# Probabilities and values of global attention as pairs of bf16 parts, with three bf16 products in place of one float32 product

## The reference

```
def global_attention(q, k, v):
    ...
    def one_block(qi):
        logits = jnp.einsum('bqkgd,bskd->bkgqs', qi, k, preferred_element_type=jnp.float32)
        p = jax.nn.softmax(logits, axis=-1)
        return jnp.einsum('bkgqs,bskd->bqkgd', p.astype(v.dtype), v)
```

## Time and profile before

| | |
|---|---|
| median of 3 runs | 2336.33 us (2333.32 to 2338.41) |
| profiled execution, its time | 2337.93 us |
| its span, first to last instruction | 2336.1 us |
| PE busy | 2272.7 us (97%) |
| DVE busy | 1623.4 us (69%) |
| ACT busy | 1223.9 us (52%) |
| POOL busy | 1090.9 us (47%) |
| mean granted clock of TensorE | 0.992 |

### The profile page before, as it was taken

How to read it: one execution, slowest core, us unless ns; L and a number is a source line. 1 busy time by engine, 2 the same in 40 slices (tenths; PEclk the granted TensorE clock), 3 DMA queues, 4 the chain that set the end, 5 groups by cost and what they waited for, 6 DMA issues and landing times.

```text
span 2336.1 us, 55145 instructions
## 1 busy us (share of the span) xinstructions
PE 2272.7 (97%) x24026; PEld 1661.3 (71%) x24026; DVE 1623.4 (69%) x1972; ACT 1223.9 (52%) x1568; POOL 1090.9 (47%) x712
## 2 busy tenths in 40 slices
PE   8999999999999999979999999999999999999997
PEld 3554677664444458779888888888888888888874
DVE  4776666583222456867887878788878878887875
ACT  4333666583111236446566555655656656665654
POOL 0000111133332215647666677667667766766642
PEclk9999999999999999999999999999999999999998
DMA  9102201503222345568899999989999998999896
GB/s 338 38 25 73 55 2 38 181 2 91 55 54 63 100 162 157 183 251 315 307 329 341 316 338 332 323 316 340 334 318 325 344 324 314 340 332 322 321 326 251
DMA packets 252440, 524.24 MB, mean 224 GB/s; under 512 B 8412, under 2 KB 57677, under 8 KB 252077
## 3 DMA queue, kind: packets, MB, share of 16 engines
q1 hardware_dynamic: 241692, 488.51, 59.3%
q0 software_dynamic: 10512, 32.25, 4.7%
HBM read 492.42 MB, written 28.31 MB: 223 GB/s over the span
## 4 chain that ended last, share of the span: by engine, by line
PE 91%; DVE 3%; ACT 2%; issue 2%; DMA 2%; SPq 0%; POOL 0%; DVEq 0%; ACTq 0%; POOLq 0%
PE ps L1855 24%; PE ps L1857 24%; PE ps L1856 24%; PE ps L2251 4%; PE ps L2039 3%; PE ps L2051 3%; PE ps L1916 3%; PE ps L1951 1%; PE ps L2187 1%; PE ps L1892 1%; ACT arena L1087 1%; DMA arena<-w_in 1%; PE ps L1989 1%; PE ps L2216 1%; PE ps L1941 1%
## 5 line engine op out<-in xcount | busy, mean ns | idle before, releaser
L1855 PE MATMUL ps<-arena 128*128 128x160 bf16 (+4 forms) x5624 | 1388.6, 266 | 10.8 <-DVE arena L1735 7.0
L1856 PE MATMUL ps<-arena 128*128 128x160 bf16 (+4 forms) x5624 | 1389.2, 266 | 0.6 <-issue 0.6
L1857 PE MATMUL ps<-arena 128*128 128x160 bf16 (+4 forms) x5624 | 1389.3, 266 | 0.0
L1392 DVE TENSOR_TENSOR arena<-arena 128x2048 bf16<-128x2048 f32 x378 | 912.4, 2418 | 225.8 <-ACT arena L974 221.2
L974 ACT ACTIVATE arena<-arena 128x2048 bf16<-128x2048 f32 x384 | 726.6, 1904 | 218.9 <-PE ps L1857 174.6
L1855 PEld LDWEIGHTS ps<-arena 128*128 128x128 bf16 x5624 | 549.1, 98 | 162.1 <-issue 16.6
L1857 PEld LDWEIGHTS ps<-arena 128*128 128x128 bf16 x5624 | 549.1, 98 | 152.9 <-issue 0.6
L1856 PEld LDWEIGHTS ps<-arena 128*128 128x128 bf16 x5624 | 549.1, 98 | 140.7 <-issue 0.3
L868 POOL TENSOR_TENSOR arena<-arena 128x320 bf16<-128x320 f32 x128 | 262.3, 2049 | 10.0
L865 POOL TENSOR_TENSOR arena<-arena,ones 128x320 bf16<-128x320 f32 x128 | 180.9, 1413 | 143.8 <-DVE arena L1735 143.4
L1245 ACT ACTIVATE arena<-ps 128x160 f32<-128x160 f32 x256 | 77.5, 303 | 300.3 <-PE ps L1857 290.1
(11 more groups left out here) (263 smaller groups left out, 2193.2 us busy)
## 6 DMA issues: line engine op xcount, KB each, us to landing
arena<-w_e_gate SPq DMA_DIRECT2D x64, 2048.0 KB, 8.5
arena<-w_e_up SPq DMA_DIRECT2D x64, 2048.0 KB, 9.9
arena<-w_e_down SPq DMA_DIRECT2D x64, 2048.0 KB, 9.2
arena<-w_ada SPq DMA_DIRECT2D x12, 2048.0 KB, 9.2
arena<-w_in SPq DMA_DIRECT2D x30, 512.0 KB, 5.3
arena<-x_sample SPq DMA_DIRECT2D x16, 512.0 KB, 3.7
arena<-w_in SPq DMA_DIRECT2D x3, 2048.0 KB, 16.5
arena<-w_out SPq DMA_DIRECT2D x2, 2048.0 KB, 8.9
```

The source lines that it names most:

```text
L1392: ve.tensor_tensor(lo, stage_half(kind, a), hi, ALU.subtract).then_inc(lo_done, 1)
L1855: pe.matmul(out, w_hi, x_hi, start=start, stop=False)
L1856: pe.matmul(out, w_hi, x_lo, start=False, stop=False)
L1857: return pe.matmul(out, w_lo, x_hi, start=False, stop=stop)
```

## The change

V of the global branch is no longer kept as float32. ACT copies keys and V of a tile together into `raw` (256 columns in one instruction where it had two of 128), and POOL makes a high bf16 part and a low one from it, the low one being what the high one leaves. ACT waits for POOL's second instruction before it overwrites `raw` in the next tile. The turned probabilities are also kept as two bf16 parts. ACT copies all pieces of an item, rounded to bf16 (the high part), and DVE subtracts that from the same PSUM bank and writes the low part. The bank is free after the subtraction. PV of the global branch is high x high, high x low and low x high, 48 bf16 products where there were 16 float32 ones. The buffers take the same room as before. The windowed branch keeps float32 (`VB`, `PTB`).

```
--- before.py
+++ after.py
@@ -291,7 +291,7 @@
         hT = at(26112, 2, KD, P)
         qT = half_words(10240, NT, 2 * NPAIR, 2 * P)
         kT = half_words(20480, 2, 2, TOK)
-        V = at(23552, 2, NT, P)
+        VA, VB = half_words(23552, NT, 2 * P), at(24832, NT, P)
         R3, R4 = 28160, 40448
         RH = 29184
         ada_slot = {c: o for c, o in enumerate([0, 4096, 10240, 14336])}
@@ -313,7 +313,7 @@
         Pb = at(41472, 2, 2, 1024)
         PbN = at(41472, 2, 2, 256)
         PbB = at(41472, 8, 386).rearrange("p (i h) w -> p i h w", h=2)
-        PTs = [at(37376, 2, 2, 8, P), at(44560, 2, 2, 3, P)]
+        PTA, PTB = half_words(37376, 4, 8, 2 * P), at(44560, 2, 2, 3, P)
         on = [at(45568, 2, 512), at(39424, 2, 512)]
         rb = [at(23040, 512), at(40448, 512)]
         biasm = at(46592, 8, 386)
@@ -417,6 +417,7 @@
         xn_ready = sem("xn_ready")
         g_done, g_free = sem("g_done"), [sem(f"g_free{n}") for n in range(5)]
         q_in, q_sqrt, qf_ready, q_high = sem("q_in"), sem("q_sqrt"), sem("qf_ready"), sem("q_high")
+        v_in, v_high, v_split, p_high = sem("v_in"), sem("v_high"), sem("v_split"), sem("p_high")
         s_done, nm_ready, e_done = sem("s_done"), sem("nm_ready"), sem("e_done")
         b_done = sem("b_done")
         pv_done, o_norm, o_split = sem("pv_done"), sem("o_norm"), sem("o_split")
@@ -542,8 +543,7 @@
 
             return (n // 2, 4 * (n % 2)) if n_parts(items[i]) == 4 else (n, 0)
 
-        def piece_vec(i, n):
-            return len(items[i][3]) > 4 and piece(i, n)[0] == 0
+        piece_no = {x[1:]: n + 1 for n, x in enumerate(x for x in steps if x[0] == "TE" and items[x[1]][0] == 0)}
 
         def narrow(i):
             return items[i][0] == 0 and len(items[i][3]) <= 4
@@ -767,6 +767,15 @@
 
             for s in steps:
                 k = s[0]
+                if k == "G":
+
+                    t = s[1]
+                    if t == 0:
+                        gp.wait_ge(bias_out, 16)
+                    gp.wait_ge(v_in, t + 1)
+                    gp.tensor_tensor(VA[:, t, 0:P], raw[:, 640:768], ones[:], ALU.mult).then_inc(v_high, 1)
+                    gp.wait_ge(v_high, t + 1)
+                    gp.tensor_tensor(VA[:, t, P:2 * P], raw[:, 640:768], VA[:, t, 0:P], ALU.subtract).then_inc(v_split, 1)
                 if k == "RB":
                     g = s[1]
                     if g:
@@ -1023,16 +1032,17 @@
                         ac.wait_ge(g_done, 3 * t + c + 1)
                         n = 3 * t + c
                         b = ps[:, n % 5]
-                        if c:
-                            v0 = 128 if c == 1 else 384
+                        if c == 1 and t:
+                            ac.wait_ge(v_split, t)
+                        if c == 2:
                             if t == 0:
                                 ac.wait_ge(bias_out, 16)
-                            ac.activation(V[:, c - 1, t, :], b[:, v0:v0 + P], ACT.Copy)
+                            ac.activation(VB[:, t, :], b[:, 384:512], ACT.Copy)
 
                         if c == 0:
                             ins = ac.activation(raw[:, 0:512], b, ACT.Copy)
                         elif c == 1:
-                            ac.activation(raw[:, 512:640], b[:, 0:P], ACT.Copy)
+                            ac.activation(raw[:, 512:768], b[:, 0:2 * P], ACT.Copy).then_inc(v_in, 1)
                             ins = ac.activation(rawB[:, :, 0, :], b[:, 256:512].rearrange("p (j d) -> p j d", j=NPAIR),
                                                 ACT.Copy)
                         else:
@@ -1086,7 +1096,7 @@
                             p_ = src = PbB[:, i % 4, hh, slice(*window(i)[1])]
                         ac.activation(p_, src, ACT.Exp, bias=nm[:, i % 4, hh:hh + 1],
                                       accum_out=den[:, i // NPAIR % 3, 2 * j + hh:2 * j + hh + 1]).then_inc(e_done, 1)
-                if k == "TE" and not piece_vec(*s[1:]):
+                if k == "TE":
                     i, n = s[1:]
                     hh, a = piece(i, n)
                     b, free = job(("T", i, n))
@@ -1095,8 +1105,11 @@
                     if i == first_b:
                         ac.wait_ge(o_split, first_b // NPAIR)
                     z = min(4, len(items[i][3]) - a)
-                    ac.activation(PTs[items[i][0]][:, i % 2, hh, a:a + z, :], b[:, 0:z * P].rearrange("p (n q) -> p n q", n=z),
-                                  ACT.Copy).then_inc(free, 1)
+                    src = b[:, 0:z * P].rearrange("p (n q) -> p n q", n=z)
+                    if items[i][0]:
+                        ac.activation(PTB[:, i % 2, hh, a:a + z, :], src, ACT.Copy).then_inc(free, 1)
+                    else:
+                        ac.activation(PTA[:, i % 2 * 2 + hh, a:a + z, 0:P], src, ACT.Copy).then_inc(p_high, 1)
                 if k == "WS":
                     m = s[1]
                     if m == 0:
@@ -1538,15 +1551,15 @@
                         ve.tensor_tensor(p_, ps[:, 2 * (i % 2):2 * (i % 2) + 2, cols], both, ALU.add).then_inc(b_done, 1)
                         ve.wait_ge(b_done, n_add(i))
                         ve.tensor_reduce(nm[:, i % 4], p_, AX.X, ALU.max, negate=True).then_inc(nm_ready, 2)
-                if k == "TE" and piece_vec(*s[1:]):
+                if k == "TE" and items[s[1]][0] == 0:
                     i, n = s[1:]
                     hh, a = piece(i, n)
                     b, free = job(("T", i, n))
-                    if i >= 2:
-                        ve.wait_ge(pv_done, i - 1)
+                    ve.wait_ge(p_high, piece_no[(i, n)])
                     z = min(4, len(items[i][3]) - a)
-                    ve.tensor_copy(PTs[0][:, i % 2, hh, a:a + z, :], b[:, 0:z * P].rearrange("p (n q) -> p n q", n=z))\
-                        .then_inc(free, 1)
+                    p_ = PTA[:, i % 2 * 2 + hh, a:a + z]
+                    ve.tensor_tensor(p_[:, :, P:2 * P], b[:, 0:z * P].rearrange("p (n q) -> p n q", n=z), p_[:, :, 0:P],
+                                     ALU.subtract).then_inc(free, 1)
                 if k == "RB":
                     g = s[1]
                     ve.wait_ge(e_done, 2 * NPAIR * (g + 1))
@@ -2046,11 +2059,18 @@
                         pe.wait_ge(*freed[job_at[(("T", i, n), 0)]])
                     if i % NPAIR == 0 and i:
                         pe.wait_ge(o_norm, i // NPAIR)
+                    if i == 0:
+                        pe.wait_ge(v_split, NT)
                     for n, kt in enumerate(kts):
-                        for hh in range(2):
-                            ins = pe.matmul(ps[hh * 64:hh * 64 + 64, 4, j * P:(j + 1) * P],
-                                            V[:, br, kt, hh * 64:hh * 64 + 64], PTs[br][:, i % 2, hh, n, :],
-                                            start=(n == 0), stop=(n == len(kts) - 1), tile_position=(0, 64 * hh))
+                        passes = ((0, 0), (0, 1), (1, 0)) if br == 0 else ((0, 0),)
+                        for x, (u, v) in enumerate(passes):
+                            for hh in range(2):
+                                d = slice(u * P + hh * 64, u * P + hh * 64 + 64)
+                                w, m = (VA[:, kt, d], PTA[:, i % 2 * 2 + hh, n, v * P:(v + 1) * P]) if br == 0 else \
+                                    (VB[:, kt, d], PTB[:, i % 2, hh, n, :])
+                                ins = pe.matmul(ps[hh * 64:hh * 64 + 64, 4, j * P:(j + 1) * P], w, m,
+                                                start=n + x == 0, stop=n == len(kts) - 1 and x == len(passes) - 1,
+                                                tile_position=(0, 64 * hh))
                     ins.then_inc(pv_done, 1)
                 if k == "OT":
                     g = s[1]
```

1 line of the change is left out of this document (added).

## The result

| | before | after |
|---|---|---|
| median | 2336.55 us (4 runs, 2333.32 to 2338.41) | 2354.81 us (4 runs, 2353.42 to 2362.12) |
| profiled execution, its span | 2336.1 us | 2352.0 us |
| PE busy | 2272.7 us | 2261.2 us |
| DVE busy | 1623.4 us | 1665.2 us |
| ACT busy | 1223.9 us | 1254.8 us |

The changed kernel takes 1.0082 times as long, with a 95% interval of 1.0070 to 1.0094. It is slower, by 18.3 us between the medians. PE is busy 11.5 us less and the kernel is 18 us slower. The forecast was 2357 us.

The account below looks back on a forecast made before the run. PE was taken to bound the kernel (91% of the chain), its wide items only 0.19 us above a loop through other engines. Terms 23.6 - 6.4 + 2 + 1 = +20.2 us gave 2357 us, range 2346 to 2370.

Parts of the forecast that it names:

- The bound: Wide items: PE is full at 5.34 us an item, beside a loop of scores, maxima and exponentials of 5.15 us.
- PV: Probabilities times V in a wide item: 48 bf16 products take 1.64 us, where the float32 ones took 1.90.
- the rival in which the two column tiles of 64 columns queue for their loads: Wide items: weight loads share one path, the 48 products take 2.79 us, the kernel 2369 us; chance 0.17.
- Copies and subtractions: Wide items: maxima queue behind DVE's subtractions, these behind ACT's copies; ordinary items 6.02 us for 5.34, +23.6 us in all.
- AR and the small products: Wide items: PE's new free time hides most of their cost, 1.2 us left of 7.6: -6.4 us.
- the end of the stage: End of the wide items: the windowed scores wait for a DVE memset behind one more low part, +1 us (0 to 2).
- The walk: Step-by-step timing of one wide item from its maxima: next maxima at 6.02 us, 0.87 after the scores have ended.
- Narrow items: Stretch from 222 to 244 us: DVE gets 16 subtractions of 256 columns, +2 us (bounds 0 and 6.6).
- V on POOL: Projection: POOL, idle before, makes V's parts and ACT drops one copy a tile; PE covers both, 0 us.
- PE sets the pace: Wide items: DVE and ACT stay clear of PE's path, so its saving shows, -6.6 us at most, 2330 us; chance 0.06.
- No change: Whole kernel: hidden AR and saved PE time cancel a walk 0.5 us too long an item, 2337 us; chance 0.06.
- The clock: Wide items: PE's pauses lower its clock in part of the stage, 2370 us and more; chance 0.06.

Follow-up runs that it names:

- V pair: Changed kernel with V as two bf16 parts but the turned probabilities as one, two products, no subtractions, copies shared by DVE and ACT as before: 2330.20 us.
- four products: Changed kernel with the low x low product added to PV of the global branch, 64 products a wide item: 2357.09 us.
- one product: Changed kernel with PV of the global branch cut to high x high, 16 products a wide item in place of 48: 2363.06 us.
- one piece ahead: Changed kernel, same instructions, with only piece 0 turned and copied ahead of the next item's scores and maxima, piece 1 behind them: 2344.34 us.
- half the low parts: Changed kernel with low parts only for hh = 0 and high x low left out for hh = 1; ACT still makes all high parts: 2347.83 us.

## Why the prediction was right

**The bound.** Right. The loop of scores, maxima and exponentials is 5.15 us, seen bare in the V pair kernel.

**PV.** 338.79 to 340.26, 1.47 us for 48 products, 31 ns each. The term was 1.64, from 31 ns and 0.15 for a change of form, which does not appear with bf16. So the rival in which the two column tiles of 64 columns queue for their loads (2369 us) is out: it needed 2.79. The prediction took 1.64 from the loads of AR, and speaks of eight; AR has 16, of which eight fall within 0.16 us and the others, four and four, within 0.13 each. The argument held. By the Trainium skill ("TensorE: Matmul & The Clock Gate", LDWEIGHTS) 64 columns load in an estimated 53 ns; at 31 ns from product to product, the loads of the two column tiles would have to overlap. The records of these loads in the trace last 110 ns each in the median, and 48 of them lie within 1.37 us, so the records do overlap.

**Copies and subtractions.** Right, and close in size: 6.02 forecast for an ordinary item, 5.98 found from maxima to maxima (5.94 to 6.04 from scores to scores); the end of a group 7.10, found 7.06 and 7.10; a group 25.28, found 25.06, so +21.8 for eight in place of +23.6. Three experiments stand behind the reason: one piece moved in the list (-0.56 us an item), half the subtractions taken away (-0.11), and two instructions of DVE added to the kernel before (+0.5 to 1.0).

**AR and the small products.** The weakest term. Of 7.6 us I left 1.2 and added 1 for the end of the stage, 2.2; found are 203.8 - 8 x 25.06 = 3.4. The maxima, which set the pace, tell the parts: the three items with AR took 7.07, 7.08 and 7.09 us from maxima to maxima, where 5.98 is ordinary. So AR and the small products cost 3.3 us and not 1.2. The end, from the last maxima (442.71) to the windowed scores (447.86), took 5.15 us, where the forecast had 4.9. The first wide item was 0.6 us shorter than an ordinary one, which the forecast did not count, and hides a part of the error. The free time of PE was right, but in two of the three places a small product for the same vector (0.9 us) falls into the item that has the AR, and 2.8 us do not fit into the 1.8 that are free. The timeline of the changed kernel, scores, the small product, AR and the next scores:

```profile
433.34 1.47 PE L1929 MATMUL ps<-arena 64*128 64x512 bf16 x12
...
434.74 1.05 PE L1974 MATMUL ps<-sel,arena 128*128 128x2 f32 x8
...
438.26 1.92 PE L1964 MATMUL ps<-arena,cS 128*32 128x512 f32 x16
...
441.19 1.47 PE L1929 MATMUL ps<-arena 64*128 64x512 bf16 x12
```

7.85 us, and 5.17 or 6.29 in the item behind it, which gets part back. The first AR has no small product beside it, and by the prediction it should have fitted but for 0.1 us. It cost the same 1.1, for another reason:

```profile
410.09 1.92 PE L1964 MATMUL ps<-arena,cS 128*32 128x512 f32 x16
...
413.35 0.63 PE L2052 MATMUL ps<-ident,arena 128*128 128x128 f32 x4 [0.76 <-DVE arena L1561]
...
413.91 1.47 PE L1929 MATMUL ps<-arena 64*128 64x512 bf16 x12
```

The result of AR takes one of the three banks of the turned pieces. So T1 at 413.35 needs the bank of piece 3, waits 0.76 us for its low part, and holds up the scores. The walk let AR through by PE's free time alone and left the banks out.

**Narrow items.** +2 forecast, +0.8 found, within the bounds; the kernels of this study that subtract there took 22.7 to 24.6 us.

**V on POOL.** Nothing found, as forecast. POOL is idle until ACT's copy comes (timeline of the changed kernel, the last tile), and ACT has gone on with other copies when the low part is done:

```profile
220.69 0.41 ACT L1045 ACTIVATE arena<-ps 128x256 f32<-128x256 f32 x1
...
221.17 0.46 POOL L776 TENSOR_TENSOR arena<-arena,ones 128x128 bf16<-128x128 f32 x1 [15.67 <-ACT arena L1045]
...
221.70 0.43 POOL L778 TENSOR_TENSOR arena<-arena 128x128 bf16<-128x128 f32 x1
```

**The sum.** +20.2 forecast, +18.3 between the medians. The errors are -1.8 for the groups, +1.2 for AR and the end, -1.2 for the narrow items. They partly cancel, so the total is a little better than its terms, and that part is luck. The terms are read from single traces, whose spans differ by 15.9 us and not by 18.3, with -1.2 ahead of the narrow items and -1.4 behind the wide ones.

**The rivals.** That PE sets the pace is out (four products, and V pair at 5.15 us with 4.4 us of work). No change is out by the interval of the result. The clock stayed at 1.00 in the wide items of the changed kernel, but it was a rival in earnest: with one product in place of three it fell.

**The faster version.** The V pair kernel, 2330.20 us, beats both, but it drops the low part of the probabilities, so their precision in that product is that of one bf16. With both parts kept, the best here is one piece ahead, 2344.34 us, still above the kernel before.

## What to carry to other kernels

A nearly full engine can hide a loop that is almost as long: measure the loop through the other engines before making the full engine faster, since their difference (0.19 us here) is all there is to win. When work moves to an engine with free time, ask what stands behind it in that engine's queue and what it waits for itself; 1.2 us more of DVE work in an item that left 1.7 us free cost 0.7 us an item in the mean of a group, and the same work with one piece placed later cost 0.1. Splitting a float32 product into bf16 parts saves on the matrix engine (1.90 to 1.47 us) and pays on the engines that make the parts.

## What the runs showed of the hardware

- Twelve score products in 2.39 us in place of 1.47 where the clock was at its lower level, after PE had been busy 4.42 of 6 us, with 1.6 us idle in one piece. With one product in place of three the clock fell five times in the wide items. With 48 products an item (about 0.9 us idle) no fall was seen there in the trace, and none in the V pair kernel (4.4 us of work in 5.15).
- Nearly the same activity was followed by either clock. At the first group end, in 250 to 256, PE was busy 4.32 us with 64 products an item, 4.23 with half the low parts and 4.21 in the changed kernel. In 256 to 260 the clock was then 0.58 and 0.57 in the first two and 1.00 in the changed kernel. That less work on PE brings the clock down is seen in all four executions of one product; a single fall in one trace says little.
- bf16 products of 128 columns with 64-column weights, in two column tiles, follow one another every 31 ns (1.47 us for 48), and 64 of them in 1.91 us every 30. The pace is the same as for 256 columns in four tiles.
